# A second mixer in one stage instead of two, in a one-core transformer kernel

## The chip, the cores and the metric

The kernel runs on one core of one Trainium2 chip. The metric is the device time of one execution in microseconds (us). The profiler records one more execution, and the trace and the profile of this document come from that one.

## What is computed

The reference runs two blocks over 256 tokens of width 1024, all in float32. The first block has two layers. Each layer is a mixer, a cross-attention over 256 memory tokens, and a feed-forward with a short convolution and a gate. The second block is another mixer and a feed-forward of 32 experts. The change is about the mixer of the second layer, which runs two independent groups over the same normalized input and projects their joined outputs:

```python
proj = xn @ cd_w_in[j]
lru_x, lru_g, m_x, m_o, m_if = split_cols(proj, CD_SIZES)     # 512 each, m_if 8
y_a = rglru_group(lru_x, lru_g, ...)   # conv4 -> two 128-blocked gate products -> a, u;
                                       # h_t = a_t h_{t-1} + u_t;  y = h * gelu(lru_g)
y_b = mlstm_group(m_x, m_o, m_if, ...) # conv4, silu; q, k, v by 4x4 blocks; 4 heads:
                                       # decayed scores (q k) -> weights -> num / max(|den|, e^-m)
                                       # y = sigmoid(m_o) * rms(h) * gain
h = h + concat(y_a, y_b) @ w_mix_out[layer]
```

The first group is called the recurrence (names `lru.`) and the second the matrix memory (names `ml.`). What they need of weights alone is `softplus(-lambda)` for the decay of the recurrence, and the 4x4 blocks of q, k and v spread into twelve 128x128 matrices (`BD`).

## The kernel before

**Layout.** Activations are held turned: 128 channels on the partitions and 256 tokens along the row, so that a 1024-wide activation is eight 128x256 pieces (`HT`, `XT`, `MIX`). A matmul loads a 128x128 weight block and streams 256 tokens. One 512-column projection unit (`cd.0`, `cd.1`, `cd_m.0`, `cd_m.1`) is 32 such matmuls in two halves; each half fills one PSUM bank (128x512), which VectorE (V) or ScalarE (S) then reads.

**Loads.** SyncE issues one DMA for each name in `LOADS`, in that order and from one queue: a unit is usually 2 MB. It goes to the next slot of a ring of four (three called ring, one in the arena; a fifth, kv, joins in the second feed-forward), and waits until the unit that was there is marked `used`. A slot whose unit TensorE still reads when it first asks for the new one is passed over. No load starts before the fourth last has landed. The `ada.n` units are weights of the second block's modulation: V multiplies them by a row (`mod_v`, four 128x1024 operations for each) in the shadow of the feed-forwards, so V and not TensorE frees their slots.

**Order.** Each engine's order is what its functions write, stage by stage, and nothing reorders it. A wait holds everything that is behind it on its engine. `P.tile` takes the next PSUM bank in turn (banks 0 to 3 before) and waits until its last reader has freed it. The keys and values of the next cross-attention (`kv_p`, units `wkv1.0` to `wkv1.3`, 16 tiles of 8 matmuls in banks 4 and 5) are a second stream: 64 steps of two matmuls, of which `P.pace` puts one ahead of each tile, `P.fill(name, n)` puts n, and `P.drain` the rest. They depend on nothing in this stage.

**The stage before** is `lru_p/s/v` and then `mlstm_p/s/v`, with a joint barrier behind each (`joined`): no engine starts the second before all three are through the first. In `lru_v` the decay constant is worked out (24 operations on 128x4 or 128x8) behind the convolution and ahead of the mark `lru.c`, for which the gate matmuls wait. In `mlstm_p` the projection of the gates' inputs (`ml.if`) stands behind both projections. The four heads run one after the other in one set of buffers (`w0_`, `w1_`, `dn`): logs of the distances on V, exponentials on S, scores times weights on V, two matmul pairs on TensorE, absolute value on S, division on V. Two matmuls of the second stream stand between the tiles of a head. The mean of squares over all four heads, its root and three products follow, then a barrier, then the down-projection `mixo1`.

Behind and ahead of the stage: `dn0` is the down-projection of the first feed-forward, in five passes over its weights; the last pass takes `dn0.4`, `dn0.5` and `dn0.6` together (48 matmuls).

Of the kernel before, what the change touches and what calls it, by code (L numbers as in the profile page):

```python
# [186 lines left out]
wq0.1 wo0.0 wo0.1 up0.0 up0.1 up0.2 up0.3 up0.4 up0.5 up0.6 up0.7 up0.8 up0.9 up0.10 dn0.0 ada.0 ada.1 dn0.1  # L187
ada.2 dn0.2 ada.3 ada.4 dn0.3 ada.5 dn0.4 dn0.5 dn0.6 cd.0 wkv1.0 cd.1 gates wkv1.1 cd_m.0 cd_m.1 cd_if wkv1.2
wkv1.3 mixo1.0 mixo1.1 wq1.0 wq1.1 wo1.0 ada.6 wo1.1 ada.7 up1.0 up1.1 up1.2 up1.3 up1.4 up1.5 up1.6 up1.7
up1.8 up1.9 up1.10 dn1.0 ada.8 dn1.1 ada.9 dn1.2 ada.10 dn1.3 ada.11 dn1.4 dn1.5 dn1.6 in2.0 in2.1 in2.2 in2.4  # L190
in2.3 in2.5 in2.6 out2.0 out2.1
# [386 lines left out]
def build(nc, dram, out):  # L578
    ctx = ExitStack()
    with ctx:  # L580
# [977 lines left out]
        AR.reset(1408)  # L1558
        XC, GA, RG_, IG, AA, UU = (AR.get(4, 256) for _ in range(6))
        AR.reset(1408)  # L1560
        XM, XCV, E4, OG, QT, KT = (AR.get(4, 256) for _ in range(6))
        Vv = AR.get(2, 512)
        BD = AR.get(12, 128)
        ip, fp, x1, cc, Mx, mm_, x2 = [AR.get(256)[0:4] for _ in range(7)]
        ho, w0_, w1_, dn = XM, AR.get(256), AR.get(256), AR.get(256)
# [5 lines left out]
        def lru_p(P):  # L1571
            P.begin("lru")
            sum_p(P, "n1")
            P.beside(kv_p(P, 1))
            P.pace = PACE[4]
            proj_p(P, "cd.0", "lru.x", xn="n1")
            proj_p(P, "cd.1", "lru.g")
            gw = P.unit("gates")[:, 0:1024].rearrange("p (g e) -> p g e", g=8)
            for g in range(2):
                for j in (0, 2):  # L1580
                    b = P.tile(f"lru.{g}{j}")
                    P.wait_ge("lru.c")
                    for q in range(2):
                        P.mm(b[:, q * 256:(q + 1) * 256], gw[:, g * 4 + j + q, :], XC[:, j + q, :], True, True,
                             sig=f"lru.{g}{j}" if q else None)
            P.fill("lru.f", FILLS[3])
            P.joined("lru.end", VSP)

        def lru_s(S):
            S.begin("lru")  # L1590
# [3 lines left out]
            for j in (0, 2):  # L1594
                b = S.tile(f"lru.g{j}")
                S.act(GA[:, j:j + 2, :], pair(b), ACT.Gelu_apprx_tanh)
                S.free(f"lru.g{j}")
            S.table(LNEXP)
            S.act(lam_a, LAM, ACT.Abs)
            S.act(lam_a, lam_a, ACT.Exp, scale=-1.0)  # L1600
            S.mark("lru.lam")
            S.wait_ge("lru.c")
            for g, dst in ((0, RG_), (1, IG)):
# [6 lines left out]
                sigm_s(S, dst, dst)  # L1610
            S.mark("lru.gates")
            S.fill("lru.f")
            S.wait_ge("lru.la")
            S.act(AA, RG_, ACT.Exp)
            S.mark("lru.a")
            S.act(RG_, RG_, ACT.Tanh)
            S.mark("lru.th")
            S.wait_ge("lru.u2")
# [3 lines left out]
            S.joined("lru.end", VSP)  # L1622

        def lru_v(V):
            V.begin("lru")
            root_v(V, "n1")
            scaled_v(V, XT, HT, gain_of("mix_g", 1), "n1")
            for j in (0, 2):
                b = V.tile(f"lru.x{j}")
                for q in range(2):  # L1630
                    jj = j + q
                    conv_v(V, XC[:, jj, :], b[:, q * 256:(q + 1) * 256], [col("lcw", 4 * k + jj) for k in range(4)],
                           col("lcb", jj))
                V.free(f"lru.x{j}")
            V.wait_ge("lru.lam")
            V.ts(lam_b, lam_a, 2.0, None, ADD, None)
            V.recip(lam_b, lam_b)
            V.tt(lam_b, lam_a, lam_b, MUL)
            V.tt(lam_c, lam_b, lam_b, MUL)
            V.ts(lam_d, lam_c, 1.0 / 15, 1.0 / 13, MUL, ADD)  # L1640
            for d in (11, 9, 7, 5, 3, 1):
                V.tt(lam_d, lam_d, lam_c, MUL)
                V.ts(lam_d, lam_d, 1.0 / d, None, ADD, None)
            V.stt(lam_d, lam_d, 2.0, lam_b, MUL, MUL)
            V.ts(lam_c, LAM, -1.0, 0.0, MUL, MAX)
            V.tt(lam_sp, lam_c, lam_d, ADD)
            V.ts(lam_sp, lam_sp, -8.0, None, MUL, None)
            V.ts(NLGB, COL[:, coff["lgb"]:coff["lgb"] + 8], -1.0, None, MUL, None)
            V.mark("lru.c")
            V.wait_ge("lru.gates")  # L1650
            V.tt(RG_, RG_, bc(lam_sp, 2, 256), MUL)
            V.mark("lru.la")
            V.wait_ge("lru.a")
            V.tt(UU, AA, AA, MUL)
            V.wait_ge("lru.th")
            V.stt(UU, UU, 1.0, RG_, ADD, MUL)
            V.ts(UU, UU, 0.0, None, MIN, None)
            V.mark("lru.u2")
            V.tt(IG, IG, XC, MUL)
            V.wait_ge("lru.sq")  # L1660
            V.tt(UU, UU, IG, MUL)
            for j in range(4):
                V.scan(XC[:, j, :], AA[:, j, :], UU[:, j, :], 0.0, MUL, ADD)
            V.tt(MIX[:, 0:4, :], XC, GA, MUL)
            V.joined("lru.end", VSP)

        def mlstm_p(P):
            P.begin("mlstm")  # L1670
            P.back("gates")
            P.pace = PACE[5]
            proj_p(P, "cd_m.0", "ml.x")
            proj_p(P, "cd_m.1", "ml.o")
            w = P.unit("cd_if")[:, 0:64].rearrange("p (k n) -> p k n", k=8)
            b = P.tile("ml.if")
            for q in range(2):
                for c in range(8):
                    P.mm(b[0:4, q * 256:(q + 1) * 256], w[:, c, q * 4:q * 4 + 4], XT[:, c, :], c == 0, c == 7,
                         sig="ml.if" if (q == 1 and c == 7) else None)  # L1680
            P.used("cd_if")
            b = P.tile("ml.ct")
            P.wait_ge("ml.m")
            for i in range(2):
                P.tr(b[:, i * 4:i * 4 + 4], cc[:, i * 128:(i + 1) * 128], ident[0:4, 0:4], sig="ml.ct" if i else None)
            for n in range(2):
                for j in (0, 2):
                    b = P.tile(f"ml.{n}{j}")
# [1408 lines left out]
```

## Time and profile before

| | us |
|---|---|
| median of three runs | 2510.01 (2509.81 to 2514.38) |
| the profiled execution, its own time | 2514.09 |
| its span, first to last instruction | 2512.2 |
| TensorE busy in the span | 2320.8 (92%) |
| VectorE / ScalarE busy | 676.0 (27%) / 373.9 (15%) |
| mean granted TensorE clock, share of full | 0.953 |

The chain of work that ended last is 81% TensorE and 11% DMA. A busy share is an average over very different stages: the last 1000 us move the experts' weights at 427 GB/s, while the stage of this document moves 100 GB/s and has TensorE idle at many short places. What the change is worth has to be read in the stage itself, 685 to 902 us into the span.

### The profile page before, as it was taken

To read this page: it belongs to the slowest core of one execution; us is meant where nothing else is said; L and a number is where in the kernel's file an instruction comes from. 1 tells how busy PE (TensorE), PEld (TensorE's weight loads), DVE (VectorE), ACT (ScalarE), POOL (GpSimd) and SP (SyncE) were. 2 spreads that over 40 slices of the span, in tenths; PEclk is the share of its full clock that TensorE was granted. 3 is DMA by queue.
4 is the path that set the end of the run, shared out by engine and by line. 5 is a ranking of instruction groups with operands and counts; after the bars stand their busy time and mean duration, and the time that the engine had idled before them with its cause. 6 is when DMAs were issued, how large, how long until landed. Compare 5 with 4: busy or idle time off the path is not lost.

```text
span 2512.2 us, 25809 instructions
## 1 busy us (share of the span) xinstructions
PE 2320.8 (92%) x10921; PEld 1515.4 (60%) x10921; DVE 676.0 (27%) x1308; ACT 373.9 (15%) x666; POOL 139.3 (6%) x199
## 2 busy tenths in 40 slices
PE   8999899999886699999998979999999999999996
PEld 5887687888675477888876853333343443333332
DVE  3444311334224323334234241111111111111112
ACT  3321122100022121100123130000001010000001
POOL 0113200000000000000000010000000100000000
PEclk9999899999998899999999779999999999999998
DMA  5210052345521333534542119999999989999994
GB/s 227 101 68 35 1 213 97 143 150 208 201 105 44 134 134 125 210 135 181 198 161 107 67 69 382 428 427 428 428 427 427 380 363 428 427 428 427 428 427 185
DMA packets 43323, 600.08 MB, mean 239 GB/s; under 512 B 5232, under 2 KB 5504, under 8 KB 6688
## 3 DMA queue, kind: packets, MB, share of 16 engines
q1 hardware_dynamic: 43200, 598.36, 58.3%
q8 instruction: 88, 1.44, 0.2%
q14 instruction: 35, 0.29, 0.0%
HBM read 597.29 MB, written 1.05 MB: 238 GB/s over the span
## 4 chain that ended last, share of the span: by engine, by line
PE 81%; DMA 11%; DVE 5%; ACT 1%; issue 1%; SPq 0%; PEldq 0%; DVEq 0%; ACTq 0%
PE pb L402 80%; DMA ring<-in_dne 6%; DMA arena<-in_gu 4%; PE pb L412 2%; DVE arena L304 1%; DVE arena L319 1%; ACT arena L363 1%; DMA ring<-in_dn 1%; DVE arena L311 0%; DVE arena L331 0%; DMA arena<-in_wkv 0%; ACT xt L363 0%; DVE arena L313 0%; SPq L533 0%; DVE arena L343 0%
## 5 line engine op out<-in xcount | busy, mean ns | idle before, releaser
L402 PE MATMUL pb<-arena 128*64 128x512 f32 (+8 forms) x2244 | 686.9, 469 | 58.5 <-DMA ring<-in_dne 34.9
L402 PE MATMUL pb<-ring,arena 128*64 128x512 f32 x1648 | 503.6, 609 | 1.2 <-DMA ring<-in_dne 1.2
L402 PEld LDWEIGHTS pb<-arena 128*64 128x64 f32 (+4 forms) x2244 | 277.3, 171 | 238.7 <-issue 200.7
L402 PE MATMUL pb<-xt,ring 128*128 128x256 f32 (+3 forms) x1744 | 385.7, 381 | 4.9 <-DVE xt L319 3.6
L402 PEld LDWEIGHTS pb<-xt,ring 128*128 128x128 f32 (+3 forms) x1744 | 325.2, 187 | 61.9 <-issue 9.0
L402 PEld LDWEIGHTS pb<-ring,arena 128*64 128x64 f32 x1648 | 162.0, 142 | 204.6 <-issue 204.6
L402 PE MATMUL pb<-kv,arena 128*64 128x512 f32 (+1 forms) x592 | 247.6, 572 | 8.6 <-DMA arena<-in_gu 6.9
L402 PEld LDWEIGHTS pb<-kv,arena 128*64 128x64 f32 (+1 forms) x592 | 81.7, 142 | 159.5 <-issue 155.6
L369 ACT ACTIVATE arena<-pb 128x512 f32<-128x512 f32 (+1 forms) x131 | 74.5, 568 | 651.2 <-PE pb L412 418.3
L304 DVE TENSOR_TENSOR mix<-pb,mix 128x512 f32<-128x512 f32 x68 | 47.1, 692 | 430.3 <-PE pb L402 430.3
L363 ACT ACTIVATE arena<-arena 128x512 f32<-128x512 f32 (+6 forms) x164 | 101.3, 617 | 324.0 <-DVE arena L319 276.3
L402 PE MATMUL pb<-xt,arena 128*128 128x256 f32 (+1 forms) x656 | 144.6, 379 | 0.0
L402 PEld LDWEIGHTS pb<-xt,arena 128*128 128x128 f32 (+1 forms) x656 | 124.7, 191 | 16.9
L402 PE MATMUL pb<-arena,ring 128*128 128x256 f32 (+1 forms) x512 | 124.9, 400 | 10.6 <-DVE small L311 6.1
L304 DVE TENSOR_TENSOR arena<-pb,arena 128x512 f32<-128x512 f32 (+5 forms) x101 | 55.8, 552 | 277.8 <-PE pb L402 241.8
L402 PEld LDWEIGHTS pb<-arena,ring 128*128 128x128 f32 (+1 forms) x512 | 98.2, 197 | 35.9 <-issue 15.5
L402 PE MATMUL pb<-mix,ring 128*128 128x256 f32 x512 | 112.5, 381 | 0.6 <-issue 0.5
L325 POOL COPY arena<-cst 128x128 f32<-128x128 f32 x16 | 4.7, 292 | 1924.3 <-DVE arena L304 1198.7
L402 PEld LDWEIGHTS pb<-mix,ring 128*128 128x128 f32 x512 | 97.7, 191 | 16.4 <-issue 3.3
L313 DVE TENSOR_SCALAR arena<-pb 128x512 f32<-128x512 f32 x36 | 24.9, 692 | 305.8 <-PE pb L402 305.8
L402 PE MATMUL pb<-memt,arena 128*128 128x512 f32 (+1 forms) x200 | 78.8, 537 | 13.4 <-DVE mix L304 12.7
L304 DVE TENSOR_TENSOR arena<-arena 128x256 f32<-128x256 f32 (+5 forms) x132 | 78.4, 594 | 39.0 <-ACT arena L363 29.1
(167 smaller groups left out, 1856.8 us busy)
## 6 DMA issues: line engine op xcount, KB each, us to landing
ring<-in_gu SPq DMA_DIRECT2D x53, 2048.0 KB, 19.3
arena<-in_gu SPq DMA_DIRECT2D x48, 2048.0 KB, 17.8
ring<-in_dne SPq DMA_DIRECT2D x46, 2048.0 KB, 15.8
kv<-in_gu SPq DMA_DIRECT2D x31, 2048.0 KB, 14.5
arena<-in_dne SPq DMA_DIRECT2D x18, 2048.0 KB, 13.0
ring<-in_up SPq DMA_DIRECT2D x13, 2048.0 KB, 7.7
ring<-in_ada SPq DMA_DIRECT2D x9, 2048.0 KB, 8.8
ring<-in_dn SPq DMA_DIRECT2D x7, 2048.0 KB, 12.1
```

Of the source, the lines that this page charges most:

```text
L304: self.e.tensor_tensor(out, a, b, op).then_inc(self.sem, 1)
L313: self.e.tensor_scalar(out, a, s1, s2, op0, op1).then_inc(self.sem, 1)
L319: self.e.scalar_tensor_tensor(out, a, s, b, op0, op1, accum_out=accum).then_inc(self.sem, 1)
L325: self.e.tensor_copy(out, a).then_inc(self.sem, 1)
L363: self.e.activation(out, a, func, bias=bias, scale=scale, accum_out=accum).then_inc(self.sem, 1)
L369: self.e.activation(out, a, ACT.Copy).then_inc(self.sem, 1)
L402: r = self.e.matmul(out, lhsT, rhs, start=start, stop=stop, skip_group_check=True)
L412: r = self.e.transpose(out, a, ident)
```

## The change

One stage `mix1` takes the place of the two, without a barrier inside or behind it. (1) The decay constant and the twelve `BD` matrices are made at the end of the first feed-forward (`mix1_early_s`, `mix1_early_v`); the gate weights and the 4x4 blocks come in at `up0.0` by DMAs of their own, to a place outside the ring. (2) `ada.4` and `ada.5` move from the first feed-forward to the second attention, and two more units from there to the second feed-forward. `wkv1.0` is loaded ahead of the `cd` units. (3) The small projection `ml.if` comes first, and the parts of both groups alternate on all three engines. (4) Heads use two buffer sets in turn, and the roots and the output are made in halves. (5) Six PSUM banks in place of four. (6) The second stream is placed by hand, with its last 28 steps behind all else.

```diff
-up0.10 dn0.0 ada.0 ada.1 dn0.1 ada.2 dn0.2 ada.3 ada.4 dn0.3 ada.5 dn0.4 dn0.5 dn0.6 cd.0 wkv1.0 cd.1 gates
-wkv1.1 cd_m.0 cd_m.1 cd_if wkv1.2 wkv1.3 mixo1.0 ...
+up0.10 ada.0 dn0.0 ada.1 dn0.1 ada.2 dn0.2 ada.3 dn0.3 dn0.4 dn0.5 dn0.6 wkv1.0 cd_if cd.0 cd_m.0 cd.1 cd_m.1
+wkv1.1 wkv1.2 wkv1.3 mixo1.0 ...
...
+        HEADS = [raw[7:10], raw[0:3]]
+        RG_, IG = (XS_[:, n * D:(n + 1) * D].rearrange("p (j t) -> p j t", j=4) for n in range(2))
+        OG = RG_
+        UU, E4 = MIX[:, 0:4, :], MIX[:, 4:8, :]
...
+        def mix1_early_v(V):
+            V.wait_ge("lru.lam")
+            log1p_v(V, lam_d, lam_a, lam_b, lam_c)
+            V.ts(lam_c, LAM, -1.0, 0.0, MUL, MAX)
...
+            V.wait_ge("load gates32")
+            for n in range(12):
+                V.tt(BD[:, n, :].rearrange("p (m e) -> p m e", e=4), bc(cst["bd"], 2, 4),
+                     bc(QKVR[:, 4 * n:4 * n + 4], 1, 32), MUL)
...
+        def mix1_p(P):
+            P.begin("mix1")
+            sum_p(P, "n1")
+            P.main = [0, 1, 2, 3, 6, 7]
+            P.beside(kv_p(P, 1))
+            P.fill("m1.f0", 4)
...
+            P.used("cd_if")
+            proj_p(P, "cd.0", "lru.x")
+            def gates():
+                P.fill("m1.f1", 2)
...
+            proj_p(P, "cd_m.0", "ml.x", after_first=gates)
+            b = P.tile("ml.ct")
+            P.wait_ge("ml.m")
...
+            proj_p(P, "cd.1", "lru.g", after_first=values)
+            P.fill("m1.f2", 2)
...
+            def two_heads():
+                P.fill("m1.f3", 4)
+                scores(1)
+                P.fill("m1.f4", 4)
+                outputs(0)
+                scores(2)
+                P.fill("m1.f5", 4)
+                outputs(1)
+            scores(0)
+            proj_p(P, "cd_m.1", "ml.o", after_first=two_heads)
+            scores(3)
+            outputs(2)
+            P.fill("m1.f6", 4)
+            mean(0)
+            P.fill("m1.f7", 4)
+            outputs(3)
+            P.fill("m1.f8", 8)
+            mean(2)
+            P.drain("m1.d")
+            P.main = [0, 1, 2, 3]
+            down_p(P, [MIX[:, c, :] for c in range(8)], "mixo1", 4, "mixo1",
+                   ready=lambda kk: "lru.mix" if kk < 4 else f"ml.mix{kk // 2 * 2 - 4}")
...
+            moved(0)
+            negative_exp(0, RG_)
+            sigm_s(S, RG_, RG_)
+            S.mark("lru.gs0")
...
+            S.act(RG_, RG_, ACT.Tanh)
+            S.mark("lru.th")
+            gelu(0)
...
+            gelu(2)
             S.wait_ge("lru.u2")
             S.act(UU, UU, ACT.Sqrt, scale=-1.0)
             S.mark("lru.sq")
             S.table(LNEXP)
...
             if n == 0:
-                mod_v(V, range(6))
+                mix1_early_v(V)
+                mod_v(V, range(4))
             else:
...
-                mod_v(V, range(8, 12))
+                mod_v(V, range(6, 12))
...
+                    F.get("gates", GW.rearrange("p g e -> p (g e)"), dram["lru_gw"])
+                    F.get("gates", QKVR, dram["ml_qkv"])
```

How the order changes is seen best in three places. The first is SyncE's queue from the last load of `up0` on, where `arena` and `ring` are slots of the same ring and `ada` units are freed by V. Before:

```order
L533 DMA ring<-in_dn 128x4096
L533 DMA arena<-in_ada 128x4096
L533 DMA ring<-in_ada 128x4096
L533 DMA ring<-in_dn 128x4096
L533 DMA ring<-in_ada 128x4096
L533 DMA arena<-in_dn 128x4096
L533 DMA ring<-in_ada 128x4096 x2
L533 DMA ring<-in_dn 128x4096
L533 DMA arena<-in_ada 128x4096
L533 DMA ring<-in_dn 128x4096
L533 DMA ring<-in_dn 128x1024
```

And of the changed kernel, from the second `dn0` unit on:

```order
L533 DMA ring<-in_dn 128x4096
L533 DMA ring<-in_ada 128x4096
L533 DMA arena<-in_dn 128x4096
L533 DMA ring<-in_ada 128x4096
L533 DMA ring<-in_dn 128x4096 x2
L533 DMA arena<-in_dn 128x1024
L533 DMA ring<-in_dn 64x1024
L533 DMA ring<-in_wkv 128x4096
L533 DMA ring<-in_cd_if 128x64
L533 DMA arena<-in_cd 128x4096
L533 DMA ring<-in_cd_m 128x4096
```

Four `ada` units in place of six stand among the `dn0` units, and the last pass's units have no `ada` between them. The second place is the start of the stage on TensorE (`xs` is the sum of squares, `memt` the second stream, `xt` a projection, `arena` alone the gates, q, k, v or a head). Before:

```order
L402 MATMUL pb<-xs,small 128x256 x8
L402 MATMUL pb<-memt,ring 128x256 x2
L402 MATMUL pb<-xt,arena 128x256 x16
L402 MATMUL pb<-memt,ring 128x256 x2
L402 MATMUL pb<-xt,arena 128x256 x16
```

Now:

```order
L402 MATMUL pb<-xs,small 128x256 x8
L402 MATMUL pb<-memt,ring 128x256 x8
L402 MATMUL pb<-xt,ring 4x256 x16
L402 MATMUL pb<-xt,arena 128x256 x32
L402 MATMUL pb<-xt,ring 128x256 x16
L402 MATMUL pb<-memt,ring 128x256 x4
L402 MATMUL pb<-arena 128x256 x8
L402 MATMUL pb<-xt,ring 128x256 x16
L412 MATMUL pb<-cst,arena 128x4 x2
```

The gates' input projection (4x256) moved from behind four half-projections to the front, and the eight gate matmuls (`arena` x8) now have three half-projections ahead of them. The third place is TensorE in the heads, where a head was followed by two matmuls of the second stream at a time. Now:

```order
L402 MATMUL pb<-xt,arena 128x256 x16
L402 MATMUL pb<-memt,ring 128x256 x8
L402 MATMUL pb<-arena,cst 128x256 x2
L402 MATMUL pb<-arena 128x256
L402 MATMUL pb<-arena 128x128
L402 MATMUL pb<-memt,ring 128x256 x8
L402 MATMUL pb<-arena 128x256
L402 MATMUL pb<-arena 128x128
L402 MATMUL pb<-arena,cst 128x256
L402 MATMUL pb<-arena,cst 128x128
```

Eight matmuls of the second stream and half of a projection now stand between the scores of one head and its outputs.

## Rows read from the trace of the kernel before

**Rows 1.** Windows: engine busy us (and instructions), granted clock, DMA share, GB/s

```profile
527.08:554.71 27.63, 27.63 (x129) 24.32 (x128) 9.99 (x20) 1.67 (x4) 0.00 (x0) 1.00 0.37 133
624.16:685.14 60.98, 56.45 (x226) 43.84 (x224) 16.88 (x27) 1.90 (x3) 0.00 (x0) 0.92 0.51 206
657.00:660.00 3.00, 3.00 (x8) 2.37 (x9) 0.00 (x0) 0.00 (x0) 0.00 (x0) 0.50 1.02 437
685.14:902.26 217.12, 160.51 (x680) 129.46 (x679) 80.86 (x161) 48.17 (x79) 0.00 (x0) 0.88 0.25 100
1169.30:1248.40 79.10, 79.10 (x353) 65.53 (x352) 26.29 (x46) 4.95 (x9) 0.00 (x0) 1.00 0.51 196
```

**Rows 2.** Waits of TensorE, 624 to 903 us: total, times, longest

```profile
PE pb L402 <- DVE mix L304: 12.7, 1, 12.7
PE pb L412 <- DVE arena L304: 12.5, 1, 12.5
PE pb L402 <- DVE arena L304: 8.5, 4, 2.9
PE pb L402 <- DMA arena<-in_wkv: 7.8, 1, 7.8
PE pb L402 <- DVE small L311: 6.1, 1, 6.1
PE pb L402 <- issue: 4.6, 2, 4.1
PE pb L402 <- DMA ring<-in_dn: 4.5, 2, 3.8
PE pb L402 <- ACT arena L363: 4.3, 1, 4.3
```

**Rows 3.** Timeline around the down-projection: start, us, engine, operation [idle before]

```profile
599.93 1.23 DVE L319 SCALAR_TENSOR_TENSOR arena<-arena 128x1024 f32<-128x1024 f32 x1
...
610.64 0.33 SPq L533 DMA_DIRECT2D ring<-in_ada  x1
...
618.57 1.23 DVE L319 SCALAR_TENSOR_TENSOR ring<-ring,arena 128x1024 f32<-128x1024 f32 x1 [8.46 <-DMA ring<-in_ada]
...
653.06 0.48 SPq L533 DMA_DIRECT2D ring<-in_dn  x1
...
656.85 28.37 PE L402 MATMUL pb<-arena,ring 128*128 128x256 f32 x96 [3.82 <-DMA ring<-in_dn]
```

**Rows 4.** DMA issues: destination, count, size, us to landing

```profile
ring<-in_cd SPq DMA_DIRECT2D x1, 2048.0 KB, 12.2
```

**Rows 5.** Timeline of VectorE: decay constant (first, last), then BD

```profile
728.40 0.17 DVE L311 TENSOR_SCALAR small<-small 128x4 f32<-128x4 f32 x1 [13.69 <-ACT small L363]
...
732.62 0.17 DVE L311 TENSOR_SCALAR small<-col 128x8 f32<-128x8 f32 x1
...
768.23 3.89 DVE L304 TENSOR_TENSOR arena<-cst,ring 128x128 f32<-128x128 f32 x12
```

**Rows 6.** Timeline of VectorE: scaled input, convolutions, the ml.if chain

```profile
691.30 4.13 DVE L319 SCALAR_TENSOR_TENSOR xt<-ht,col,arena 128x256 f32<-128x256 f32 x8
...
702.71 0.54 DVE L313 TENSOR_SCALAR arena<-pb,col 128x256 f32<-128x256 f32 x1 [7.27 <-PE pb L402]
...
704.84 0.55 DVE L313 TENSOR_SCALAR arena<-pb,col 128x256 f32<-128x256 f32 x1
...
809.24 0.98 DVE L311 TENSOR_SCALAR arena<-pb,col 4x256 f32<-4x256 f32 x2 [13.96 <-PE pb L402]
...
822.16 0.41 DVE L304 TENSOR_TENSOR arena<-arena 4x256 f32<-4x256 f32 x1
```

**Rows 7.** Timeline of ScalarE: a table load and the 128x1024 tanh behind it

```profile
757.01 1.28 ACT L363 ACT_TABLE_LOAD   x1
...
758.30 1.06 ACT L363 ACTIVATE arena<-arena 128x1024 f32<-128x1024 f32 x1
```

**Rows 8.** Timeline of VectorE: the reciprocal in a head

```profile
853.72 1.75 DVE L331 RECIPROCAL arena<-arena 128x256 f32<-128x256 f32 x1
```

More of the change, by code:

```diff
@@ L186 @@
 ab_small ab.0 ab.1 ab.2 ab_r.1 ab_r.0 ab_r.2 rw_scratch wkv0.0 wkv0.1 wkv0.2 wkv0.3 mixo0.0 mixo0.1 wq0.0
[L187 to L191, printed above, removed]
+wq0.1 wo0.0 wo0.1 up0.0 up0.1 up0.2 up0.3 up0.4 up0.5 up0.6 up0.7 up0.8 up0.9 up0.10 ada.0 dn0.0 ada.1 dn0.1
+ada.2 dn0.2 ada.3 dn0.3 dn0.4 dn0.5 dn0.6 wkv1.0 cd_if cd.0 cd_m.0 cd.1 cd_m.1 wkv1.1 wkv1.2 wkv1.3 mixo1.0
+mixo1.1 wq1.0 wq1.1 wo1.0 ada.4 wo1.1 ada.5 up1.0 up1.1 up1.2 up1.3 up1.4 up1.5 up1.6 up1.7 up1.8 up1.9 up1.10
+ada.6 dn1.0 ada.7 ada.8 dn1.1 ada.9 dn1.2 ada.10 dn1.3 ada.11 dn1.4 dn1.5 dn1.6 in2.0 in2.1 in2.2 in2.4 in2.3
+in2.5 in2.6 out2.0 out2.1
 """
@@ L1593, in lru_s, with moved, negative_exp @@
             S.beside(kv_s(S, 1))
[L1594 to L1603, printed above, removed]
+            S.reach("ml.if")
+            S.wait_ge("free ml.if")
+            S.act(x1, fp, ACT.Abs)
+            S.act(x1, x1, ACT.Exp, scale=-1.0)
+            S.mark("ml.ef")
+            def moved(j):
+                b = S.tile(f"ml.x{j}")
+                S.copy(XM[:, j:j + 2, :], pair(b))
+                S.mark(f"ml.xm{j}")
+            def negative_exp(g, dst):
                 for j in (0, 2):
@@ L1615, in lru_s @@
             S.mark("lru.a")
+            S.wait_ge("ml.cv")
+            S.act(E4, XCV, ACT.Exp, scale=-1.0)
+            sigm_s(S, E4, E4)
+            S.mark("ml.sx")
             S.act(RG_, RG_, ACT.Tanh)
             S.mark("lru.th")
+            gelu(0)
+            for i in range(2):
+                b = S.tile(f"ml.v{i}")
+                S.copy(Vv[:, i, :], b)
+                S.free(f"ml.v{i}")
+            gelu(2)
             S.wait_ge("lru.u2")
@@ L1621, in lru_s @@
             S.table(LNEXP)
[L1622 to L1665, printed above, removed]
@@ L1746, in mlstm_s, with weights @@
                     S.free(f"ml.{n}{j}")
-            for i in range(2):
-                b = S.tile(f"ml.v{i}")
-                S.copy(Vv[:, i, :], b)
-                S.free(f"ml.v{i}")
-            for hd in range(4):
+            def weights(hd):
+                w0_, w1_, dn = HEADS[hd % 2]
                 b = S.tile(f"ml.b{hd}")
@@ L1763, in mlstm_s, with gate @@
-            S.mark("ml.sq")
-            rsqrt_s(S, E4, QT, KT, "ml")
-            S.fill("ml.d")
-            S.joined("ml.end", VSP)
-        def mlstm_v(V):
-            V.begin("mlstm")
-            place = V.unit("gates")
-            for n in range(12):
-                V.tt(BD[:, n, :].rearrange("p (m e) -> p m e", e=4), bc(cst["bd"], 2, 4),
-                     bc(place[:, 1024 + 4 * n:1028 + 4 * n], 1, 32), MUL)
-            V.used("gates")
-            for j in (0, 2):
+            def gate(j):
+                b = S.tile(f"ml.o{j}")
+                S.act(OG[:, j:j + 2, :], pair(b), ACT.Exp, scale=-1.0)
+                S.free(f"ml.o{j}")
```

345 lines of the change are left out of this document (198 added, 147 removed).

## The prediction

> **What bounds the kernel now.** I read the windows first. From the first matmul of the stage's norm to the first of `mixo1` pass 217.1 us; TensorE is busy in 160.5 of them, at a mean granted clock of 0.88, while V is busy 81, S 48, and DMA a quarter of its share [rows 1]. No engine is full: waits and their clock set the time. The list of TensorE's waits says which: 12.7 us for V's last product at the joint barrier, 12.5 for the `ml.if` chain, 8.5 for scores in the four heads, 7.8 for a `wkv` unit, 6.1 for the decay constant, 4.3 for the square, 4.6 for no cause the profile shows (4.1 of it at the start, where the scaled input is not there yet); 4.5 for `dn` units lie ahead of the stage [rows 2]. Without those last it is 56.5 us idle.
>
> **What the stage needs at least.** Two feed-forward units of 32 matmuls take 27.63 us at clock 1.00 [rows 1], 0.4317 us for a 256-column matmul. The stage has, in such units, 8 (norm) + 128 (second stream) + 128 (projections) + 16 (`ml.if`) + 8 (gates) + 8 (q, k) + 4 (v) + 4 x 6.5 (heads) + 4 (means) = 330, so 142.5 us, before and after alike. The 18.0 us between that and 160.5 busy are half-clock stretches behind the waits and small bubbles. After 3.8 us of idle the clock stood at 0.50, 1.2 GHz [rows 1, 3].
>
> **The down-projection ahead of it.** Passes 3 to 5 of `dn0` are 112 matmuls, 48.35 us; they took 60.98 [rows 1]. The last small unit was issued only at 653.06, when pass 4 was through and freed its slot, since an `ada` unit stood between; TensorE waited 3.8 us, and the last pass then took 28.37 us where 48 matmuls need 20.7 [rows 3]. Now two `ada` units fewer are in the way: `dn0.4` takes the slot of `ada.2`, and `dn0.5` and `dn0.6` are issued at the end of pass 3, one pass ahead. What is new is V's early part ahead of `mod_v`: 4.4 us for the constant (728.40 to 732.79) and 3.9 for `BD` [rows 5]. V began `mod_v` at 599.93 [rows 3], behind a 1.3 us product that moves to the attention; so it begins at 607.0 and frees `ada.0` 5.1 us later (four operations at 1.27 us from start to start), at 612.1. Behind that wait in SyncE's queue stands `dn0.2`, free since 610.6. A second load right behind another landed in 12.2 us [rows 4], one alone in 7.9 (610.64 to 618.57) [rows 3]; so `dn0.2` lands at 624.7. TensorE wants it two passes of 13.8 us and a 0.7 us stall before 653.03, at 624.7. I take 0.5 us of stall; the upper bound is another load's 4.3 us ahead of it plus half-clock time. Gain here 60.98 - 48.35 - 0.5 = 12.1.
>
> **The stage, step by step** (t from its first matmul). Norm to 3.5; first second-stream tile to 6.9, where TensorE idled before. The scaled pieces come at 7.2 to 10.3 (691.30 + 4.13 ends at 695.43) [rows 6]: `ml.if` follows them one by one, 0.8 us lost, done at 14.7. V's chain on it took 809.24 to 822.57, 13.3 us [rows 6], so V is free at 28.0; a convolution of 256 columns takes 2.13 (702.71 to 704.84) [rows 6], four for `lru.c`: 36.5. TensorE meanwhile does `cd.0` (28.5), half of `cd_m.0` (35.4) and two steps: it asks for `lru.c` at 37.1. **Slack 0.6.** The 12.5 us and 6.1 us waits are gone.
>
> Then both groups' evictions alternate. S has four table loads in the stage where it had five, but in one row: tanh, gelu, sqrt and back. A load and its tanh took 757.01 to 759.36 with nothing between [rows 7], 1.28 and 1.06. With 128x512 evictions I get the gelus at 60.0 and 64.1, the root at 66.4, the table at 67.7 and the q and k copies at 70.6. TensorE has the first head's distances at 69.6 and wants the scores: **1.0 us of stall**. V ends the recurrence at 75.9 and the first weights at 77.5; they are wanted at 86.7. The recurrence's products and the four scans, the 12.7 us wait of before, lie behind `cd_m.1`.
>
> Heads: outputs of head 0 at 88.1; S's absolute value to 88.6; V's maximum, reciprocal (1.75) [rows 8] and product to 91.4; weights of head 1 to 93.0, wanted at 93.1: **slack 0.1**. Later ones have more: 99.3 against 103, 109.2 against 112.2, and the squares are in time by 3 us. The last mean ends at 121.4, and 28 steps (24.2 us) of the second stream follow, while V needs some 4 us for the second half's root and product: the tail of root, products and barrier is covered with 20 us to spare. If that cover were gone, these 4 us would show.
>
> Loads: `wkv1.0` comes a pass ahead; `cd_if`, `cd.0`, `cd_m.0` are issued at t = 0 (`cd.0` wanted at 14.7, within 12.2). `wkv1.0` holds a slot until 86.7, so `wkv1.2` and `wkv1.3` are issued only then, wanted at 117 and 131. Nothing is late; the 7.8 us wait goes.
>
> Two estimates remain. TensorE loses some tenths wherever 4-row weights and short groups alternate; no row isolates it. From below it is nothing, from above the 18.0 us, most of which I have as clock. I take 2.0, near the lower end. And with no gap over 1.1 us, the clock stays full, as it does over 79.1 us of `dn1` [rows 1]. Stage: 142.5 + 0.8 + 1.0 + 2.0 = 146.3, a gain of 70.8.
>
> Priced at nothing: the gate loads issued at `up0.0` (SyncE waits there anyhow for a slot), the condition's product in the first attention (V waits 1.2 us more ahead of evictions which TensorE wants later), two more `ada` units in the second feed-forward. The last is 8 x 1.27 = 10.2 us of V in 79.1 us in which it is busy 26 [rows 1]; five slots are there, and each `dn1` unit is issued a pass or more ahead.
>
> **Sum.** 12.1 + 70.8 = 82.9. From the profiled execution's 2514.09 this gives 2431.2, from the median, 4.1 lower, 2427.1. I say **2430**. Later stages shift as a whole: the experts' loads start when mixer slots come free, so nothing downstream holds a fixed time.
>
> The Trainium skill, "ScalarE: Activation LUTs", What ACT_TABLE_LOAD costs, puts a set switch at 1.28 us plus a drain of 1.38. By that the sqrt and the way back would end 2.8 later, and the scores would stall 3.8 in place of 1.0. This trace has no drain between load and tanh [rows 7], so the sum goes by the row.
>
> **Rivals.** (A) *Thin spots fail.* `lru.c`, the q and k copies and the second head's weights have 0.6, -1.0 and 0.1 us. If each comes 3 us later, as a queue of many handoffs may, there are three gaps of 3 to 4 us with some 3 us of half clock behind each (of the 18.0, over five or six gaps of before): about 20 us, so 2450. For it: the old heads left TensorE idle four times [rows 2]. Against it: now 3.5 us or more of other work stands in each place. (B) *The early part delays `dn0.2`.* 4.3 us of stall plus up to 7.7 us lost as in the last pass of before [rows 3], 12 in all: 2442. (C) *The second feed-forward gives it back.* If one of its units comes behind an `ada` as `dn0.6` did, 3.8 + 7.7 = 11.5 us: 2441. Before there was no wait there at all [rows 1]. (D) *The clock, and slower than before.* If the many short groups in six banks kept TensorE's clock at 0.50 for the stage, its 142.5 us would double: 2572. It decides from 82.9 / 142.5 = 58% of the stage at half clock. Against it: the clock fell behind gaps, not within runs. The Trainium skill, "TensorE: Matmul & The Clock Gate", A second HAM failure mode, describes such a thing: short idles between groups that cycle through banks make the clock swing. It would make this rival's time. (E) *No change*: TensorE's lost waits come back as waits for loads in the same stage, since a slot is held long. It would need some 80 us of them, and DMA is at a quarter of its share [rows 1].
>
> **Chances.** Forecast 0.62; A 0.17, B 0.09, C 0.07, D 0.02, E 0.03. The floor is no loss at all: 2510 - 74.6 - 12.6 = 2423. The likeliest case alone has 2423 to 2442. The range has to leave out at most 2 in 10: 2422 to 2453, which holds A, B and C. Within 0.2% (5 us, what a measurement of this kernel can tell) of no change: E, 0.03. Slower: D, 0.02. Faster: 0.95.
>
> **What would show it.** TensorE idle under 5 us and clock at 1.00 in a stage of 145 to 150 us; the last pass of `dn0` in 21 us without a wait; no wait for `dn1`. Wrong would be: waits of over 2 us for S or V behind the gates, the q and k tiles or head 1; a wait for `dn0.2`; a clock under 0.95 in the stage.

## The result, and the profile after

The changed kernel's median is 2434.66 us (2432.0 to 2436.07, four runs) beside 2511.33 (2509.81 to 2514.38) for the kernel before on the same chip: 0.9692 of its time, with a 95% interval of 0.9675 to 0.9709. 76.7 us are gone, where the prediction had 82.9. The profiled execution took 2433.32 us (span 2431.5), and the granted clock over the span is 0.963 where it was 0.953.

The windows of the changed kernel: passes 3 to 5 of `dn0`, the stage (first matmul of its norm to the first of `mixo1`), the 2 us in which its one wait ends (at 748.55), and `dn1`. The columns are those of [rows 1].

```profile
624.56:677.06 52.50, 51.74 (x227) 41.22 (x225) 7.82 (x13) 1.89 (x3) 0.00 (x0) 1.00 0.43 171
677.06:825.67 148.61, 147.02 (x679) 122.44 (x679) 72.44 (x131) 46.74 (x78) 0.00 (x0) 0.99 0.37 142
748.00:750.00 2.00, 1.45 (x5) 1.30 (x6) 1.86 (x3) 1.52 (x4) 0.00 (x0) 0.57 0.00 0
1091.70:1170.90 79.20, 79.20 (x354) 65.53 (x352) 36.16 (x62) 4.93 (x9) 0.00 (x0) 1.00 0.63 249
```

The stage fell from 217.1 to 148.6 us, with V busy for 8.4 us less than before (its weight-only part went ahead of the stage) and S for 1.4 less. TensorE's waits between the start of pass 3 and `mixo1`, all that there are, where [rows 2] had eight groups:

```profile
PE pb L402 <- ACT arena L363: 1.4, 1, 1.4
PE pb L402 <- DMA arena<-in_dn: 0.8, 1, 0.8
```

TensorE's timeline, with what it did around both waits (start, length, operation, tile, shapes, count, and in brackets the idle time ahead):

```profile
625.58 14.08 PE L402 MATMUL pb<-arena 128*128 128x256 f32 x64 [0.76 <-DMA arena<-in_dn]
...
652.66 2.54 PE L402 MATMUL pb<-arena,ring 128*128 128x256 f32 x11
655.04 0.59 PE L402 MATMUL pb<-arena 128*128 128x256 f32 x2
655.56 2.62 PE L402 MATMUL pb<-arena,ring 64*128 64x256 f32 x10
658.02 0.59 PE L402 MATMUL pb<-arena 128*128 128x256 f32 x2
658.54 2.62 PE L402 MATMUL pb<-arena,ring 64*128 64x256 f32 x10
...
677.06 3.72 PE L402 MATMUL pb<-xs,small 128*128 128x256 f32 x16
680.62 3.62 PE L402 MATMUL pb<-memt,ring 128*128 128x256 f32 x16
684.37 7.51 PE L402 MATMUL pb<-xt,ring 128*4 128x256 f32 x32
...
714.36 3.62 PE L402 MATMUL pb<-arena 128*128 128x256 f32 x16
...
748.55 1.62 PE L402 MATMUL pb<-arena 128*128 128x256 f32 x4 [1.42 <-ACT arena L363]
...
762.35 0.92 PE L402 MATMUL pb<-arena 128*128 128x256 f32 x4
...
801.50 24.34 PE L402 MATMUL pb<-ring,memt 128*128 128x256 f32 x112
825.67 13.98 PE L402 MATMUL pb<-mix,arena 128*128 128x256 f32 x64
```

The counts here are of instructions; a matmul of this document is two of them. The last pass of `dn0` is to be seen in its pattern of 2.98 us (655.56 to 658.54) for six matmuls, of which one has weights of 64 rows. The four-instruction score group at 748.55 took 1.62 us, the next head's at 762.35 took 0.92: the first ran at half clock. Behind the last mean, at 801.50, the reserved steps run 24.3 us without a gap.

SyncE's queue, where the wait for `dn0.2` arose: the `ada` unit is issued when V frees its slot, and the `dn0` unit right behind it.

```profile
612.62 0.33 SPq L533 DMA_DIRECT2D ring<-in_ada  x1
613.07 0.36 SPq L533 DMA_DIRECT2D arena<-in_dn  x1
```

VectorE, at the two places where the stage hangs on it: where it reads `ml.if`, and the last convolutions ahead of the gates at 714.36.

```profile
691.92 0.98 DVE L311 TENSOR_SCALAR arena<-pb,col 4x256 f32<-4x256 f32 x2 [4.57 <-PE pb L402]
...
712.42 1.52 DVE L319 SCALAR_TENSOR_TENSOR arena<-pb,col,arena 128x255 f32<-128x255 f32 x3
```

The convolutions end at 713.94, 0.4 us before the gates begin. ScalarE, ahead of the one wait: the load of the set for the square root, the root, and the copies of q and k for which the scores wait.

```profile
741.61 1.28 ACT L363 ACT_TABLE_LOAD   x1
742.90 1.06 ACT L363 ACTIVATE mix<-mix 128x1024 f32<-128x1024 f32 x1
...
747.12 1.28 ACT L363 ACTIVATE arena<-pb 128x512 f32<-128x512 f32 x2
```

### The profile page after: what moved, and what is told of

It reads as the page before. It is cut to its first block, busy times and chain, and to the rows that moved or that the text cites. A ratio compares the mean times of both kernels' runs of the same rounds, so it can differ in the third digit from the quotient of the medians.

```text
span 2431.5 us, 25823 instructions
## 1 busy us (share of the span) xinstructions
PE 2298.3 (95%) x10921; PEld 1509.8 (62%) x10921; DVE 674.6 (28%) x1312; ACT 372.6 (15%) x668; POOL 138.9 (6%) x199
## 4 chain that ended last, share of the span: by engine, by line
PE 83%; DMA 11%; DVE 3%; ACT 1%; issue 1%; SPq 0%; PEldq 0%; DVEq 0%; ACTq 0%
PE pb L402 81%; DMA arena<-in_dne 7%; DMA arena<-in_gu 4%; PE pb L412 2%; DVE arena L304 1%; DVE arena L319 1%; DMA arena<-in_dn 1%; ACT arena L363 0%; DVE arena L311 0%; ACT xt L363 0%; DMA col<-in_cols 0%; DVE ring L319 0%; SPq L533 0%; DVE xs L304 0%; ACT L363 0%
## 5 line engine op out<-in xcount | busy, mean ns | idle before, releaser
L402 PE MATMUL pb<-arena 128*64 128x512 f32 (+10 forms) x2340 | 705.0, 464 | 16.4 <-DVE arena L304 9.2
L402 PE MATMUL pb<-ring,arena 128*64 128x512 f32 x1648 | 480.2, 595 | 8.3 <-DMA arena<-in_gu 6.9
L402 PE MATMUL pb<-xt,ring 128*128 128x256 f32 (+3 forms) x1808 | 402.4, 383 | 5.1 <-DVE xt L319 3.6
L402 PE MATMUL pb<-kv,arena 128*64 128x512 f32 (+2 forms) x592 | 264.6, 603 | 37.7 <-DMA arena<-in_dne 35.4
L363 ACT ACTIVATE arena<-arena 128x512 f32<-128x512 f32 (+4 forms) x151 | 86.4, 573 | 299.4 <-DVE arena L319 272.0
L402 PE MATMUL pb<-xt,arena 128*128 128x256 f32 (+1 forms) x528 | 115.9, 378 | 0.0
L402 PEld LDWEIGHTS pb<-xt,arena 128*128 128x128 f32 (+1 forms) x528 | 99.7, 190 | 13.8 <-issue 0.4
L402 PE MATMUL pb<-arena,ring 128*128 128x256 f32 (+1 forms) x432 | 100.4, 385 | 0.0
L402 PEld LDWEIGHTS pb<-arena,ring 128*128 128x128 f32 (+1 forms) x432 | 80.0, 189 | 17.9 <-issue 8.0
L369 ACT ACTIVATE memt<-pb 128x512 f32<-128x512 f32 x38 | 22.7, 597 | 409.0 <-PE pb L402 409.0
## 6 DMA issues: line engine op xcount, KB each, us to landing
ring<-in_dne SPq DMA_DIRECT2D x32, 2048.0 KB, 13.7
```

The costliest lines, as they stand in the source:

```text
L363: self.e.activation(out, a, func, bias=bias, scale=scale, accum_out=accum).then_inc(self.sem, 1)
L369: self.e.activation(out, a, ACT.Copy).then_inc(self.sem, 1)
L402: r = self.e.matmul(out, lhsT, rhs, start=start, stop=stop, skip_group_check=True)
```

## Experiments

The twelve kernels ran in three groups of four, each group on one chip with its own runs of the kernel before (medians 2513.77, 2512.47, 2512.99). Ratios are to those; a pair of numbers in brackets behind a ratio is its 95% interval. From `mixo1`'s first matmul to the end, the profiled executions of all kernels of this document take 1602.7 to 1610.6 us. 2.7 us of that belong to the edit that splits the down-projections and so shortens `dn1` there too, and 1.6 to the half clock that `e_tail_bare` carries into `mixo1`; with both taken out, 1605.4 to 1609.9 are left, so where an edit touches the stage alone, its windows say more than the medians. "The stage" is always from the norm's first matmul to `mixo1`'s. Unless another is named, an edit is made in the changed kernel.

**What moving the `ada` units does alone** (`e_before_ada`): the kernel before, with the new places of the `ada` loads, in both feed-forwards and the second attention, and nothing else.

```diff
-up0.10 dn0.0 ada.0 ada.1 dn0.1 ada.2 dn0.2 ada.3 ada.4 dn0.3 ada.5 dn0.4 dn0.5 dn0.6 cd.0 ...
+up0.10 ada.0 dn0.0 ada.1 dn0.1 ada.2 dn0.2 ada.3 dn0.3 dn0.4 dn0.5 dn0.6 cd.0 ...
...
-                mod_v(V, range(6))
+                mod_v(V, range(4))
...
-                mod_v(V, range(8, 12))
+                mod_v(V, range(6, 12))
```

> The kernel before with one part of the change alone: four ada units in place of six between the dn0 units, and six in the second feed-forward, with the load order of the change there; the mixer is untouched. My theory (the time is TensorE's work plus its own waits, each with its own cause): the wait of 3.8 us for the last dn0 unit and the half-clock pass behind it go, and passes 3 to 5 take 52.0 us (the changed kernel's 52.5 less a wait of 0.8, plus nothing) where they took 61.0; the mixer stage stays at 217 us and the second feed-forward's down-projection at 79.2. Sum -9 us, 2502. Rival (the wait moves into the stage: the units for the mixer are loaded behind the same queue and come late instead): 2508 to 2511, with a new wait at the start of the stage. Rival (it is given back in the second feed-forward): a wait of 3 to 4 us for a dn1 unit there and 2508 to 2515.

The median was 2503.54 us (2501.49 to 2506.36), 0.9958 [0.9941, 0.9974]. The windows row of passes 3 to 5:

```profile
625.09:676.47 51.38, 51.38 (x226) 41.11 (x224) 6.32 (x11) 1.89 (x3) 0.00 (x0) 1.00 0.38 139
```

They have no wait and full clock, and the stage takes 216.8 us with its old waits. So 9.6 of the 60.98 us come back by the loads alone. What stays open is that the passes are 3.0 us over 48.35 though nothing waits: the cause is neither a load nor the clock.

**Where those 3 us of `dn0` went** (`e_passes`, `e_before_passes`): the three last units taken in three passes, in the changed kernel and in the kernel before.

```diff
-            down_p(P, FBLOCKS, ..., merged=3)
+            down_p(P, FBLOCKS, ..., merged=1)
```

> The changed kernel with the three last dn0 units, and the three last dn1 units, in a pass each instead of one pass together. The last pass of dn0 took 23.6 us for 48 matmuls at full clock, 2.98 us for each six, where 0.4317 us each is 2.59; I had put 20.7 into the sum. Theory (each change from the 64-row weights of the last unit to 128-row weights costs 0.33 to 0.39 us, since the trace has a gap of 0.33 us in the weight loads there, and there are eight in each down-projection): with one such change in place of eight both feed-forwards gain 2.5 to 2.9 us, 5 to 6 in all, 2429. Rival (48 matmuls with 64-row weights among them cost that whatever the order, or the sooner end of the last pass exposes the residual and the squares by as much): within 1.5 us of the changed kernel.

The median was 2427.77 us (2425.29 to 2430.24), 0.9663 [0.9649, 0.9676]. Its windows row for passes 3 to 7 (the same 112 matmuls), and TensorE's weight loads near their end:

```profile
626.31:675.04 48.73, 48.73 (x224) 42.41 (x224) 7.01 (x11) 1.29 (x3) 0.00 (x0) 1.00 0.50 194
```

```profile
667.63 3.43 PEld L402 LDWEIGHTS pb<-arena 128*128 128x128 f32 x16
671.39 3.32 PEld L402 LDWEIGHTS pb<-arena,ring 64*128 64x128 f32 x16 [0.33 <-issue]
```

The same view of the changed kernel, where one 64-row weight stands in each six:

```profile
655.56 0.29 PEld L402 LDWEIGHTS pb<-arena,ring 64*128 64x128 f32 x2 [0.33 <-issue]
656.18 1.59 PEld L402 LDWEIGHTS pb<-arena,ring 128*128 128x128 f32 x8 [0.33 <-issue]
657.80 0.41 PEld L402 LDWEIGHTS pb<-arena 128*128 128x128 f32 x2
658.54 0.29 PEld L402 LDWEIGHTS pb<-arena,ring 64*128 64x128 f32 x2 [0.33 <-issue]
```

At each change between 128-row and 64-row weights, in either direction, the weight loader stands for 0.33 us. The merged pass has eight such pairs of changes and the split one has one; the seven fewer are the 2.75 us that this edit saves (51.48 to 48.73, and 48.73 is 0.38 over the 48.35 of full weights). `dn1` gains 2.7 likewise. Another 1.5 us came from the stage, which took 147.07 us; nothing that the profile shows ties it to the passes, and the last section comes back to it. In the kernel before the same edit gave more:

> The kernel before with only the last three units of the two feed-forwards' down-projections in a pass each. If a switch of weights from 64 rows to 128 costs 0.33 to 0.39 us wherever it stands, this gains 5 to 6 us here too: 2505 to 2508. The wait of 3.8 us for the last dn0 unit may also fall, since two small units are there a pass sooner: down to 2502. Rival: no difference that can be measured.

The median was 2497.72 us (2496.79 to 2500.19), 0.9937 [0.9922, 0.9953]: 15.3 us less, and below the 2502 that I had put lowest. Its passes 4 to 7:

```profile
638.80 34.99 PE L402 MATMUL pb<-arena,ring 128*128 128x256 f32 x160 [0.73 <-DMA ring<-in_dn]
```

`dn0.6` now lands while the passes ahead of its own still run; the 3.8 us wait of [rows 3] and its half clock are gone with the order of loads untouched. From the start of pass 3 (624.09) to the norm (673.72) are 49.6 us, 11.3 less than before; `dn1` gives 2.7 (76.4 for 79.1). What the change gains at `dn0` could be had, and more, by this one number.

**The early part** (`e_early_back`): decay constant and `BD` made in the stage again, on V behind the recurrence's convolutions and ahead of the mark `lru.c`, for which the gates wait.

```diff
             S.beside(kv_s(S, 1))
+            mix1_early_s(S)
...
                 V.free(f"lru.x{j}")
+            mix1_early_v(V)
             V.mark("lru.c")
...
-                mix1_early_s(S)
...
-                mix1_early_v(V)
```

> The changed kernel with the weight-only part (24 small operations and twelve for BD, 8.3 us of VectorE) put back into the stage, behind the first group's convolutions and ahead of the mark lru.c. My theory (the ml.if chain and the convolutions leave a slack of 0.6 us at lru.c): TensorE waits 7 to 8 us for it at the gate matmuls, with 2 to 3 us of half clock behind, while the 0.8 us wait for dn0.2 goes; +8 to +10 us against the changed kernel, so 2443 to 2445. Rival (work put in the feed-forward was no cost in the stage, since VectorE has room there): +0 to +2 us, 2433 to 2437.

The median was 2444.06 us (2441.74 to 2446.13), 0.9718 [0.9702, 0.9734]. The stage took 158.42 us (+9.8), and beside the 1.4 us of the changed kernel TensorE had a new wait in it, at the gates, with half clock behind it (5.16 us for the 3.62 of the changed kernel):

```profile
721.89 5.16 PE L402 MATMUL pb<-arena 128*128 128x256 f32 x16 [7.97 <-DVE arena L304]
```

It had none for `dn0.2`: with V free earlier, the unit was in time. To have this part early therefore costs 0.76 us at `dn0` and saves 9.8 in the stage.

**The order of `ml.if`** (`e_if_late`): the small projection behind `cd.0` and all of `cd_m.0`, and its chains on V and S behind the recurrence's convolutions and the first of the matrix memory's.

```diff
-dn0.6 wkv1.0 cd_if cd.0 cd_m.0 cd.1 ...
+dn0.6 wkv1.0 cd.0 cd_m.0 cd_if cd.1 ...
```

> The changed kernel with the gates' input projection and its chain on VectorE and ScalarE put back behind the projection cd_m.0, where the transposes wait for it. Theory (12.5 us of waits of before were this chain's 13.3 us with nothing of TensorE's beside it): TensorE waits 13 to 14 us ahead of the transposes, 2 us of half clock behind, while up to 1 us at the start goes; stage 162 to 165 us, 2448 to 2452. Rival (the chain is hidden by the woven order wherever it stands): under 5 us more.

The median was 2448.35 us (2447.27 to 2453.91), 0.975 [0.9735, 0.9764]; the stage took 162.34 us, 13.7 more. That is the 13.3 us of V's chain [rows 6], all of it now in front of TensorE. There are also 0.8 us for `cd.0` at the start and the 1.4 at the scores as in the changed kernel, and TensorE's busy time is 0.4 us less, since there is half clock behind the new wait and none behind the scores:

```profile
739.08 0.34 PE L412 MATMUL pb<-cst,arena 4*128 4x4 f32 x2 [13.52 <-DVE arena L304]
```

**Two buffer sets or one** (`e_one_set`): all heads in the first set, the distances of a head made behind the outputs of the one ahead of it.

```diff
-        HEADS = [raw[7:10], raw[0:3]]
+        HEADS = [raw[7:10], raw[7:10]]
...
             weights(0)
+            outputs(0)
             distances(1)
-            outputs(0)
...
```

> The changed kernel with one set of buffers for all heads: the distances of a head are taken after the outputs of the head before it. My theory (what stands between the heads on TensorE now covers the exchange with VectorE and ScalarE, whichever the number of sets): a wait of 1 to 2 us for the weights of head 1, none or under 1 us for heads 2 and 3; +1 to +4 us against the changed kernel, 2436 to 2439. Rival (the two sets are what removed the 8.5 us of waits in the heads): waits of 8 us or more in the heads and half clock behind them, +8 to +14 us, 2443 to 2449.

The median was 2433.93 us (2432.06 to 2440.66), 0.9678 [0.9662, 0.9695], not to be told from the changed kernel's; the stage took 150.15 us (+1.5), with one wait more, and it is short:

```profile
779.06 0.92 PE L402 MATMUL pb<-arena 128*128 128x256 f32 x4 [1.14 <-DVE arena L304]
```

The second set is worth next to nothing: the halves of `cd_m.1` and the steps between the heads already cover one head's chain.

**The placed steps** (`e_even_pace`): one step ahead of each tile in place of the placed ones, `wkv1.1` ahead of `cd_m.1`.

```diff
+            P.pace = 1
...
-                P.fill("m1.f3", 4)
+                P.fill("m1.f3", 0)      # and so for f1 to f8
```

> The changed kernel with the second stream dealt evenly, as before: 4 steps at the start, then one ahead of each tile, the rest in the drain (wkv1.1 is loaded one place earlier, as TensorE asks for it earlier). My theory (placement matters only where the slack is thin): with some 7 steps fewer (6 us) between the scores of head 0 and the outputs of head 1, waits of 2 to 5 us for the weights of heads 1 to 3 and for the squares in all, +4 to +10 us with half clock, 2438 to 2445. Rival (any filling does, since the same 64 steps are there): within 2 us of the changed kernel, 2433 to 2437.

The median was 2441.9 us (2439.12 to 2444.99), 0.9717 [0.97, 0.9733]; the stage took 154.82 us (+6.2), with none of the 1.4 us at the first scores but waits of 0.47 and 2.64 us in the heads and 2.94 at the second mean. The last is

```profile
805.38 2.04 PE L402 MATMUL pb<-mix,cst 128*128 128x512 f32 x2 [2.94 <-ACT mix L363]
```

and that mean runs at half clock behind it (2.04 us; 1.12 in `e_fill`, below).

**The tail cover** (`e_tail_bare`): all steps left, the eight and the last 28, are done ahead of the outputs of the last head, none behind them.

```diff
             P.fill("m1.f7", 4)
+            P.drain("m1.d")
             outputs(3)
-            P.fill("m1.f8", 8)
+            P.fill("m1.f8", 0)
             mean(2)
-            P.drain("m1.d")
```

> The changed kernel with the end of the second stream (8 steps and the last 28) ahead of the outputs of head 3, so nothing covers the last division, square, mean, root and product. My prediction said that 4 us would show if the cover were gone. Theory now: TensorE waits some 3.5 to 4 us for the last squares and then 1 to 2 us of half clock, but mixo1 does not wait, since its first pass of 13.8 us reads only the recurrence's half of MIX; the stage +4 to +6 us, 2439 to 2441. Rival (the whole tail shows: squares, root and product): a further wait of 3 to 4 us in front of or in mixo1, +9 to +12 us.

The median was 2440.82 us (2438.94 to 2441.54), 0.971 [0.9695, 0.9725]; the stage took 153.83 us (+5.2). The 1.4 us are as they were; the new wait is ahead of the second mean, and none is behind it:

```profile
827.35 2.08 PE L402 MATMUL pb<-mix,cst 128*128 128x512 f32 x2 [3.90 <-ACT mix L363]
829.22 15.55 PE L402 MATMUL pb<-mix,arena 128*128 128x256 f32 x64
```

The first pass of `mixo1` reads other pieces and needs 14 us (15.55 here, since it begins at half clock), and so it hides root and product by itself. What showed is the way from the last head's outputs to its squares. The size of the wait was as the prediction had it, the part it named was not.

**Steps ahead of the first scores** (`e_fill`): four of the eight steps behind `outputs(3)` put ahead of `scores(0)`, where TensorE waits 1.42 us for the q and k copies.

```diff
+            P.fill("m1.f9", 4)
             scores(0)
...
             outputs(3)
-            P.fill("m1.f8", 8)
+            P.fill("m1.f8", 4)
```

> The changed kernel with four more steps of the second stream ahead of the scores of head 0 and four fewer behind the outputs of head 3. TensorE waited 1.42 us there for ScalarE's q and k copies, and the matmuls behind that ran at clock 0.57 for 4 us. Theory: the wait and the half clock go, and nothing else waits, -1.4 -1.8 = -3 us in the stage, 145.5 us, 2431.5. Rival (the wait only moves, to the squares of heads 2 and 3, which have 3 us of slack less now): the stage keeps 148 to 149 us.

The median was 2431.39 us (2429.72 to 2434.92), 0.9673 [0.966, 0.9687]; the stage took 146.31 us, 2.3 less. The wait at the scores is gone and the clock stayed full there; one of 0.44 us is new, at the second mean, which has four steps less ahead of it. The medians of `e_fill` and of the changed kernel do not part them; the windows do, for one execution each.

**Four banks** (`e_four_banks`): `P.main = [0, 1, 2, 3]` also in the stage.

> The changed kernel with four PSUM banks for the tiles of the stage in place of six. Theory (the evictions are interleaved over three engines with waits of up to 5 us between a tile's end and its reading, which four banks do not hold): ml.x2 has to wait for the convolutions to free an earlier bank, and the gate tiles for ScalarE; waits of 5 to 15 us in all, 2440 to 2452. Rival (banks are no limit): within 1.5 us of the changed kernel.

The median was 2437.24 us (2431.94 to 2439.14), 0.9701 [0.9686, 0.9715]; the stage took 149.32 us (+0.7). It has four waits of 1.24, 0.32, 1.03 and 0.68 us (at the gates, at the first head's distances and its scores, and at a later head's scores), 3.27 us in all where the changed kernel has 1.42, and no half clock behind them. So 0.7 us is too kind to four banks: beside `e_passes`, whose clock stayed full in the stage as well, they cost 2.3 us (149.32 and 147.07, one execution each). I had expected waits of 5 to 15 us, and that was wrong: when the groups alternate, most evictions end before their bank is wanted again.

**The changed kernel again** (`e_after`, no edit), beside

**the edits that paid, together** (`e_best`): three passes, four steps ahead of the first scores, two steps more at the head of the stage (f0 from 4 to 6), and the early part of V behind the first `mod_v` units instead of ahead of them.

```diff
-            P.fill("m1.f0", 4)
+            P.fill("m1.f0", 6)
...
+            P.fill("m1.f9", 4)
             scores(0)
...
-            P.fill("m1.f8", 8)
+            P.fill("m1.f8", 4)
...
-            down_p(P, FBLOCKS, ..., merged=3)
+            down_p(P, FBLOCKS, ..., merged=1)
...
-                mix1_early_v(V)
                 mod_v(V, range(4))
+                mix1_early_v(V)
```

> The changed kernel itself, beside the next three on the same chip. 2434 to 2435, stage 148.6 us; where the runs of one kernel spread by some 5 us, so must these.

> The changed kernel with what the runs so far point to: the last three down-projection units in a pass each in both feed-forwards (-6), four steps of the second stream ahead of the scores of head 0 (-2.3), six steps at the start of the stage in place of four, so that the scaled input is complete when ml.if begins (-0.4), and the weight-only part behind the four ada units of the first feed-forward, so that it holds no load back (-0.6). Theory (all four are separate waits of TensorE, and add up): -9 us against the changed kernel, 2425 to 2427, stage 146. Rival (they overlap, or the later ml.if chain makes lru.c late, by 1.7 us at most): 2428 to 2430.

`e_after` took 2434.32 us (2432.35 to 2436.44), 0.9686 [0.9672, 0.9699], with a stage of 148.74 and the same wait (1.43 us). `e_best` took 2423.12 us (2422.61 to 2427.87), 0.9649 [0.9636, 0.9662], 11.2 us below `e_after` on the same chip and 2 us below what I had put lowest. It beats both kernels. The stage gave 3.1 us of it, the down-projections some 5.5, the wait for `dn0.2`, which is gone, 0.5; the other 2 lie ahead of `dn0`'s pass 3 and behind `mixo1`, where other kernels that are the same there differ by as much. Its stage, and the one wait that is left:

```profile
672.94:818.60 145.66, 145.22 (x679) 121.42 (x679) 72.45 (x131) 47.34 (x79) 0.00 (x0) 1.00 0.36 139
```

```profile
795.20 1.13 PE L402 MATMUL pb<-mix,cst 128*128 128x512 f32 x2 [0.44 <-ACT mix L363]
```

## Why the prediction came out

It was right: 2434.7 was measured where 2430 stood, within 2422 to 2453, and in the main for the reasons that it gave. By the profiled executions (80.8 us less) the account is: stage 217.12 to 148.61, 68.5 (70.8 predicted); passes 3 to 5 of `dn0` 60.98 to 52.50, 8.5 (12.1 predicted); the rest, 3.8, is 4.1 from `mixo1` on and -0.4 ahead of `dn0`'s pass 3. The 4.1 lie within the 4.5 us by which this part differs between kernels, so I don't count them as a gain of the change; no run settles it, and of the eleven executions with the new mixer nine take 1605.4 to 1607.3 us there, while the three with the old one take 1609.3 to 1609.9. The two terms of the sum thus came to 77.0 and not to 82.9, both too large, and that the profiled execution lies so near to its 2431.2 is luck by these 3.8. The medians differ by 4.1 us less than the profiled executions do: that of before was 2.8 above its median, that of the changed kernel 1.3 below.

- **The floor of the stage.** 330 matmuls at 0.4317 us, 142.5 us, held: `e_best` has 145.66 with a wait of 0.44. Waits and their clock were all of the rest but some 3 us.
- **`dn0`: a mis-sized term.** "the last pass then took 28.37 us where 48 matmuls need 20.7": they take 23.6, since a switch between 64-row and 128-row weights costs some 0.39 us a pair, which the 0.4317 us from full weights does not hold. So 12.1 was too much by 3.1, and by 0.3 more for the stall (0.76, not 0.5), and the sign that it named, a last pass in 21 us, did not come. The same error stands in the reading of before: of the 7.7 us over in its last pass, some 3 were never the clock's. `e_passes` and `e_before_passes` showed it.
- **The wait for `dn0.2`.** V's early part ahead of `mod_v` holds SyncE's queue up to 612.62 and 613.07; predicted 612.1. With the early part gone there was no wait. The prediction had 0.5 us of stall in its sum and yet listed a wait for `dn0.2` as a sign of being wrong; its sum is what held.
- **The stage's 146.3.** Measured 148.6. The q and k copies stalled TensorE by 1.42 us (1.0 predicted), `lru.c` had 0.4 us of slack (0.6). The half clock behind that wait was not in the sum. It is worth 1.5 to 1.7 us: the stage took 148.61 and 148.74 with it (`e_after`), and 147.07 in `e_passes` with the same wait and full clock. The step "with no gap over 1.1 us, the clock stays full" put this term at nothing; the gap came out as 1.4, and the clock fell in five of the seven executions that had it. What is left over 142.5, 1.4 and 1.7 is 3.0, where 2.8 was put (0.8 for the scaled input, 2.0 for switching). How that splits was not tried.
- **The tail.** "these 4 us would show": 3.9 showed as a wait, 6.8 with the half clock behind it (5.2 in the stage, 1.6 in `mixo1`), but for the squares, not for root and product.
- **Loads.** No unit of the stage was waited for.
- **The table switch.** The scores stalled 1.42 us, and the root began at 742.90, right behind the 1.28 us load at 741.61: no drain here. By what the Trainium skill, "ScalarE: Activation LUTs", What ACT_TABLE_LOAD costs, adds for a drain (1.38 us a switch, here two), they would have stalled 3.8, as an estimate.
- **Rivals.** A (thin spots): two of three held, the third cost 1.4 and its clock. `e_even_pace` comes nearer to it, with 6.1 us of waits in three places. B: the mechanism is real and cost 0.76 us, not 12. C: `dn1` took 79.20 us without a wait, with V at 36.2 busy for 26. D: the clock was 0.99 over the stage. What that rival took from the Trainium skill ("TensorE: Matmul & The Clock Gate", A second HAM failure mode) did not occur with six banks in turn; the page tells of a clock that swings between the two levels, so a stage at half clock throughout, 2572 us, was more than it says. E: no load wait took the place of the others.

Which part of the change gives what, by undoing one at a time: the `ada` move 9.6 us (at `dn0`, done alone on the kernel before), `ml.if` first 13.7, the early part 9.8, placed steps 6.2, the cover at the end 5.2 (it is a part of the placing), the second buffer set 1.5, two more banks 0.7 (2.3 at equal clock). These are not a sum, as each was taken with the others in place; they come to some 41 of the 77 us. The rest I put down to the alternation of the two groups without a barrier, which no run took out by itself. Of the waits in [rows 2], the 12.7 us for V's last product, the 7.8 for the `wkv` unit and the 4.1 at the start are gone, and no run here shows by which part of the change.

## What to carry to other kernels

Work out what a stage needs from its matmul count and one undisturbed row, and take the difference to its time as the prize; then look which single chain TensorE waits for at each place, and put that chain's first instruction (here the small `ml.if`) ahead of the large independent work. Independent matmuls are worth most where a known chain ends: the same 64 steps spread evenly cost 6.2 us here. More buffers and banks gave little once the order was right. Price a run of matmuls by a row with the same weight shapes: one partial block among full ones costs more than its share, and a load that is too late for a merged pass may be in time if the pass is split.

## What the runs showed that was not expected

**The clock behind a short wait is not settled by the wait.** In the changed kernel, `e_after`, `e_one_set` and `e_tail_bare`, TensorE waited 1.42 or 1.43 us at the first scores and then ran at half clock at once; in `e_passes` it waited as long at the same place, with the same work of the stage ahead, and stayed at full clock. The 2 us that begin with the group behind the wait, in `e_after`:

```profile
749.20:751.20 2.00, 1.99 (x6) 1.73 (x7) 1.93 (x3) 1.08 (x3) 0.00 (x0) 0.51 0.00 0
```

and in `e_passes`:

```profile
746.50:748.50 2.00, 1.96 (x10) 1.81 (x11) 1.93 (x3) 1.11 (x3) 0.00 (x0) 1.00 0.00 0
```

Six matmul instructions against ten in the same time, at 1.2 and at 2.4 GHz. `e_if_late` stayed full there too. In `e_early_back` the first microsecond behind the wait was at full clock, and then it fell while TensorE was busy without a gap:

```profile
757.62 0.89 PE L402 MATMUL pb<-arena 128*128 128x256 f32 x4 [1.43 <-ACT arena L363]
```

```profile
759.20:761.20 2.00, 2.00 (x7) 1.56 (x6) 1.93 (x3) 0.00 (x0) 0.00 (x0) 0.50 0.00 0
```

What decides it the runs leave open. It is worth 1.5 to 1.7 us here, by the stage of `e_passes` beside those of the changed kernel and `e_after`:

```profile
675.04:822.11 147.07, 145.48 (x679) 121.43 (x679) 72.43 (x131) 47.34 (x79) 0.00 (x0) 1.00 0.36 138
```

So a comparison of two stages here can hold 1.5 us that is not the edit's.

**Weights of 64 rows** next to weights of 128 leave the weight loader standing 0.33 us at each switch, in and out, and TensorE loses 0.39 us by the pair. Sixteen loads of 64 rows one behind the other have the pause once.
